# A fused transformer layer with 32 experts on one core: landing places for two down units instead of one gate-up unit, and the expert of fewest tokens processed last

## The reference

```python
logits = (xt @ p['w_router']).astype(F32) + p['b_router'].astype(F32)
topv, topi = lax.top_k(logits, TOP_K)
wts = jax.nn.softmax(topv, axis=-1)
...
gu = xb @ p['w_gu'][e] + p['b_gu'][e]
gate = jnp.minimum(gu[:, :D_FF], SWIGLU_LIMIT)
up = jnp.clip(gu[:, D_FF:], -SWIGLU_LIMIT, SWIGLU_LIMIT)
act = (up + 1.0) * gate * jax.nn.sigmoid(SWIGLU_ALPHA * gate)
return (act @ p['w_down'][e] + p['b_down'][e]).astype(F32) * w[:, None]
```

## Time and profile before

| | us |
|---|---|
| median of 3 runs | 1631.74 (1631.41 to 1634.96) |
| the profiled execution | 1629.55, span 1627.9 |
| PE, DVE, ACT, POOL busy | 1403.2, 624.3, 247.6, 183.9 |
| DMA | 505.66 MB, mean 311 GB/s |

### The profile page before, as it was taken

The page is one execution under the profiler, slowest core; times in us unless marked ns, Lnnn a source line. Parts: engine busy times, 40 slices in busy tenths (PEclk is TensorE's granted clock), DMA queues, the critical chain, the costliest instruction groups (busy, mean ns, idle before and its releaser), DMA issues.

```text
span 1627.9 us, 40564 instructions
## 1 busy us (share of the span) xinstructions
PE 1403.2 (86%) x16361; PEld 758.5 (47%) x16362; DVE 624.3 (38%) x1321; ACT 247.6 (15%) x580; POOL 183.9 (11%) x240
## 2 busy tenths in 40 slices
PE   6998989999999699979999797797779797779794
PEld 3445656367676445535554353343335343334352
DVE  2334646344623534334344242332314332233334
ACT  2124532211110311101111010000001010000011
POOL 2021310000000001000110110110110110001100
PEclk9999989988999699989999898898989898899897
DMA  9734992940191379699999999999999969997940
GB/s 356 247 137 151 356 396 72 369 150 1 46 351 69 155 307 408 266 402 423 406 395 403 428 414 417 417 406 415 414 424 407 413 283 393 423 407 295 384 183 33
DMA packets 71426, 505.66 MB, mean 311 GB/s; under 512 B 6528, under 2 KB 6648, under 8 KB 35316
## 3 DMA queue, kind: packets, MB, share of 16 engines
q1 hardware_dynamic: 63588, 480.98, 73.1%
q0 software_dynamic: 7792, 24.08, 4.5%
HBM read 499.92 MB, written 5.11 MB: 310 GB/s over the span
## 4 chain that ended last, share of the span: by engine, by line
PE 72%; DMA 17%; DVE 6%; issue 1%; ACT 1%; POOL 1%; SPq 1%; DVEq 0%; ACTq 0%; POOLq 0%
PE psum L533 67%; DMA region<-in_w_gu 13%; DMA ring<-in_w_down 2%; PE psum L697 2%; DMA ring<-in_w_ada 2%; PE psum L1018 1%; PE psum L993 1%; DVE region L1315 1%; POOL ring L2208 1%; DMA ring<-in_w_gu 1%; DVE region L1164 1%; PE psum L729 0%; ACT region L1819 0%; DVE region L1282 0%; SPq L2273 0%
## 5 line engine op out<-in xcount | busy, mean ns | idle before, releaser
L533 PE MATMUL psum<-ring,region 128*32 128x256 f32 (+2 forms) x11264 | 744.6, 390 | 138.1 <-POOL ring L2208 134.1
L533 PEld LDWEIGHTS psum<-ring,region 128*32 128x32 f32 (+1 forms) x11264 | 370.5, 112 | 460.2 <-POOL ring L2208 165.6
L1819 ACT ACTIVATE region<-psum 128x256 f32<-128x256 f32 (+5 forms) x330 | 136.7, 417 | 1149.5 <-PE psum L533 503.6
L533 PE MATMUL psum<-region 128*32 128x256 f32 (+11 forms) x2700 | 253.2, 424 | 19.1 <-DVE region L1208 9.0
L2208 POOL COPY ring<-region 128x1024 f32<-128x1024 f32 x124 | 123.8, 1041 | 919.7 <-DMA region<-in_w_gu 744.4
L1729 DVE TENSOR_TENSOR region<-region,psum 128x1280 f32<-128x1280 f32 x110 | 163.2, 1484 | 165.8 <-PE psum L533 165.8
L533 PE MATMUL psum<-region,ring 128*128 128x320 f32 (+1 forms) x640 | 170.3, 421 | 1.4 <-DVE region L1570 1.4
L1699 DVE TENSOR_SCALAR region<-psum,region 128x320 f32<-128x320 f32 x55 | 30.3, 551 | 355.7 <-PE psum L533 355.7
L533 PEld LDWEIGHTS psum<-region 128*32 128x32 f32 (+5 forms) x2700 | 101.5, 138 | 129.3 <-issue 91.8
L533 PEld LDWEIGHTS psum<-region,ring 128*128 128x128 f32 x640 | 117.2, 193 | 48.8 <-issue 5.5
L1685 DVE TENSOR_SCALAR region<-region 128x32 f32<-128x32 f32 x168 | 34.7, 266 | 106.0 <-issue 106.0
(11 more groups left out here) (301 smaller groups left out, 769.5 us busy)
## 6 DMA issues: line engine op xcount, KB each, us to landing
ring<-in_w_gu SPq DMA_DIRECT2D x97, 2048.0 KB, 11.3
ring<-in_w_down SPq DMA_DIRECT2D x64, 2048.0 KB, 11.3
region<-in_w_gu SPq DMA_DIRECT2D x31, 2048.0 KB, 17.3
ring<-in_w_ada SPq DMA_DIRECT2D x12, 2048.0 KB, 13.8
ring<-in_w_in SPq DMA_DIRECT2D x11, 2048.0 KB, 19.3
ring<-in_cache_k SPq DMA_DIRECT2D x64, 256.0 KB, 5.0
ring<-in_cache_v POOLq DMA_DIRECT2D x64, 256.0 KB, 5.2
ring<-in_w_out SPq DMA_DIRECT2D x2, 2048.0 KB, 21.3
```

Of the source, the lines that this page charges most:

```text
L533: return pe.matmul(out, lhsT, rhs, start=start, stop=stop, skip_group_check=True)
L1819: return act.activation(out, src, ACT.Copy)
```

## The change

- `LANDINGS` becomes 2, and the landing places are those of the two down units (4 and 5) instead of quarter 0. The second place lies in space of the router's scratch; the tiles that live on beside it are laid out below it.
- SP's order for an expert becomes: quarters 0, 1, 2 and 3 of this expert into the ring, each behind its wait, then for each down unit a wait until GpSimd has moved all four pieces of *this* expert's unit, and the fill of the *next* expert's. Its first fill of the second place waits for the last readers of the scratch.
- TensorE waits for quarter 0 as for the others (one semaphore, no pieces) and before each down unit for that unit's fourth piece.
- GpSimd copies two units an expert, eight pieces instead of four.
- The expert with fewest tokens among experts 2 to 31 is processed last; those behind it move up by one. For this DVE finds the least count, makes a step number for each expert, TensorE turns it, and the running sums are made in the new order; lists `AT_STEP` (step of a block, for the semaphore counts) and `AT_ORDER` (expert of a step, for SP's loads) are added.
- SP reads three registers an expert instead of one.

```diff
-LANDINGS = 1
+LANDINGS = 2
...
+        landing = [region[:, REGION + KT * NT - UNIT:REGION + KT * NT], Area(E.at).take(UNIT)]
...
-            pe.wait_ge(blocks_ready, 1)
+            pe.wait_ge(steps_ready, 1)
+            out = claim(pe, ALLB, "steps")
+            mm(out[0:NE, 0:NE], ones[0:1, 0:NE], step_row[0:1, 0:NE], True, True)
+            mm(out[0:NE, NE:NE + 1], step_row[0:1, 0:NE], ones[0:1, 0:1], True, True)\
+                .then_inc(full_sem("steps"), 1)
+            pe.wait_ge(reached_ready, 1)
...
             def gate_up_quarter(c, expert):
 
-                if c >= LANDINGS:
-                    pe.wait_ge(unit_landed[moe_slot[c]], 16 * expert + (landed_base[c] + 16))
+                pe.wait_ge(unit_landed[moe_slot[c]], 16 * expert + (landed_base[c] + 16))
...
-                        if c < LANDINGS:
-                            pe.wait_ge(piece_moved[c], PIECES * expert + (2 * j + q + 1))
...
             def down(expert):
                 for half in range(2):
                     i = 4 + half
-                    pe.wait_ge(unit_landed[moe_slot[i]], 16 * expert + (landed_base[i] + 16))
+                    pe.wait_ge(piece_moved[half], PIECES * expert + PIECES)
...
+            step(dve.memset(least_row[0:1, :], -4.0 * NT))
+            dve.tensor_scalar(least_row[0:1, 2:NE], pp[0:1, 162:160 + NE], -1.0, None, ALU.mult)
...
+            step(dve.max(least8[0:1, :], least_row[0:1, :]))
+            step(dve.max_index(least_ix[:], least8[0:1, :], least_row[0:1, :]))
+            step(dve.tensor_copy(step_row[0:1, 2 * NE:2 * NE + 1], least_ix[:, 0:1]))
+            least = step_row[0:1, 2 * NE:2 * NE + 1]
+            step(dve.scalar_tensor_tensor(step_row[0:1, 0:NE], iota[0:1, 0:NE], least, iota[0:1, 0:NE],
+                                          ALU.is_gt, ALU.subtract))
+            step(dve.tensor_scalar(step_row[0:1, NE:2 * NE], iota[0:1, 0:NE], least, -float(NE),
+                                   ALU.is_equal, ALU.mult))
+            step(dve.tensor_tensor(step_row[0:1, 0:NE], step_row[0:1, 0:NE], step_row[0:1, NE:2 * NE], ALU.add))
+            dve.tensor_scalar(step_row[0:1, 0:NE], step_row[0:1, 0:NE], -1.0, float(NE - 1), ALU.mult, ALU.min)\
+                .then_inc(steps_ready, 1)
+            dve.wait_ge(*own(steps_ready))
+            dve.wait_ge(*full("steps"))
+            step(dve.tensor_copy(step_of[0:NE, 0:1], bank("steps")[0:NE, NE:NE + 1]))
+            dve.tensor_scalar(reached[0:NE, 0, :], bank("steps")[0:NE, 0:NE], step_of[0:NE, 0:1], None, ALU.is_ge)
...
                 for i in range(LANDINGS):
-                    pool.wait_ge(unit_landed[moe_slot[i]], landed_base[i] + 16)
-                    pool.wait_ge(unit_read[i], before)
+                    pool.wait_ge(unit_landed[moe_slot[4 + i]], landed_base[4 + i] + 16)
+                    pool.wait_ge(unit_read[4 + i], before)
                     pool.wait_ge(landing_filled[i], filled)
...
-                sp.dma_start(landing[i], gu[expert, i].rearrange("o p f -> p (o f)")).then_inc(landing_filled[i], 16)
+                sp.dma_start(landing[i].rearrange("p (c f) -> p c f", c=2),
+                             dn[expert, i].rearrange("o p c f -> p (o c) f")).then_inc(landing_filled[i], 16)
...
-                    elif i < LANDINGS:
+                    elif i >= RING - LANDINGS:
                         continue
...
+            for m in range(KT):
+                sp.wait_ge(*drained("bd", m))
+            sp.wait_ge(weight_rows_ready, 1)
+            fill_landing(1, slice(1, 2))
             with sp.Fori(1, NE - 1) as e:
                 before = sp.value_load(ints[0:1, bass.ds(e + (AT_BLOCKS - 1), 1)], min_val=1,
                                        max_val=MAX_BLOCKS)
-                expert_weights(bass.ds(e, 1), before)
+                this = sp.value_load(ints[0:1, bass.ds(e + AT_ORDER, 1)], min_val=0, max_val=NE - 1)
+                after = sp.value_load(ints[0:1, bass.ds(e + (AT_ORDER + 1), 1)], min_val=0, max_val=NE - 1)
+                expert_weights(bass.ds(this, 1), before)
                 for i in range(LANDINGS):
                     sp.wait_ge(piece_moved[i], PIECES * e + PIECES)
-                    fill_landing(i, bass.ds(e + 1, 1))
+                    fill_landing(i, bass.ds(after, 1))
```

More of the change, by code:

```diff
@@ L65 @@
 AT_ROUND = AT_LATER + 1
-N_INTS = AT_ROUND + N_LIST
+AT_STEP = AT_ROUND + N_LIST
+AT_ORDER = AT_STEP + N_LIST
+N_INTS = AT_ORDER + NE
 def const_pack():
@@ L265, in build @@
         selwT = E.take(NT)
+        pos = E.take(3, ROUNDS * NE)
         E.at = max(E.at, fin_at + KT * NT + 2 * FF)
         late_const = E.take(n_const - n_late)
+        wts = E.take(3, NE)
+        fin_ss = E.take(6)
+        fin_rstd = E.take(3)
+        plan_row = E.take(N_LIST)
+        fin_gain = E.take(D)
+        landing = [region[:, REGION + KT * NT - UNIT:REGION + KT * NT], Area(E.at).take(UNIT)]
         logits = E.take(3, NE)
         mask = E.take(3, NE)
-        wts = E.take(3, NE)
         eq = E.take(3, NE)
@@ L286, in build @@
         begun = E.take(N_LIST)
[L287 to L290, removed]
+        active = E.take(N_LIST)
+        least_row = E.take(NE)
+        least8 = E.take(8)
+        step_row = E.take(2 * NE + 1)
+        step_of = E.take(3)
+        reached = E.take(3, NE)
         x1_sq = Area(REGION - KT * NT).take(KT, NT)
-        landing = [region[:, REGION + KT * NT - UNIT:REGION + KT * NT]]
         assert E.at <= REGION - KT * NT
-        pos = E.take(3, ROUNDS * NE)
+        assert E.at <= REGION + KT * NT - UNIT
         y_out = h2_tok
         top_ix = sb("top_ix", [P, 3, 8], U32)
+        least_ix = sb("least_ix", [1, 8], U32)
         spare = hmT[:].rearrange("p h t -> p (h t)").bitcast(BF16)
@@ L936, in _ @@
             for i in range(3):
-                last = mm(out[0:NE, 128:129], mask[:, i, :], ones[:, 0:1], i == 0, i == 2)
+                mm(out[0:NE, 128:129], mask[:, i, :], ones[:, 0:1], i == 0, i == 2)
+            for i in range(3):
+                last = mm(out[0:1, 160:160 + NE], ones[:, 0:1], mask[:, i, :], i == 0, i == 2)
             last.then_inc(full_sem("pos"), 1)
@@ L968, in _ @@
             mm(out[0:1, 0:N_LIST], ones[0:NE, 0:1], begun[0:NE, :], True, True)
-            mm(out[0:1, P:P + N_LIST], plan[0:NE, 0:1], begun[0:NE, :], True, True)\
+            mm(out[0:1, P:P + N_LIST], plan[0:NE, 0:1], begun[0:NE, :], True, True)
+            mm(out[0:1, 2 * P:2 * P + N_LIST], const("number", NE), active[0:NE, :], True, True)\
                 .then_inc(full_sem("list"), 1)
@@ L1653, in _ @@
             step(dve.tensor_reduce(plan[0:NE, 1:2], plan[0:NE, 2:1 + ROUNDS], AX, ALU.add))
-            dve.tensor_scalar(plan[0:NE, 0:1], plan[0:NE, 1:2], 1.0, None, ALU.add).then_inc(blocks_ready, 1)
-            dve.wait_ge(*own(blocks_ready))
+            step(dve.tensor_scalar(plan[0:NE, 0:1], plan[0:NE, 1:2], 1.0, None, ALU.add))
+            step(dve.max(least8[0:1, :], least_row[0:1, :]))
[13 more added lines that the diff above has]
+            dve.tensor_scalar(reached[0:NE, 0, :], bank("steps")[0:NE, 0:NE], step_of[0:NE, 0:1], None, ALU.is_ge)
+            dve.tensor_scalar(reached[0:NE, 1, :], iota[0:NE, 0:NE], step_of[0:NE, 0:1], None, ALU.is_ge)\
+                .then_inc(free_sem("steps"), 1)
+            dve.wait_ge(*drained("steps"))
+            dve.tensor_scalar(reached[0:NE, 2, :], iota[0:NE, 0:NE], step_of[0:NE, 0:1], None, ALU.is_equal)\
+                .then_inc(reached_ready, 1)
+            dve.wait_ge(*own(reached_ready))
             dve.tensor_copy(split_f32[:, NT:2 * NT], bank("wT")[0:3 * NE, 0:NT]).then_inc(free_sem("wT"), 1)
@@ L1663, in _ @@
             dve.wait_ge(*drained("cum"))
+            step(dve.tensor_tensor(step_of[0:NE, 2:3], plan[0:NE, 1:2], plan[0:NE, 0:1], ALU.subtract))
+            step(dve.tensor_scalar(active[0:NE, :], iota[0:NE, 0:N_LIST], step_of[0:NE, 2:3], None, ALU.is_ge))
+            step(dve.scalar_tensor_tensor(active[0:NE, :], iota[0:NE, 0:N_LIST], plan[0:NE, 1:2], active[0:NE, :],
+                                          ALU.is_lt, ALU.mult))
             dve.tensor_scalar(begun[0:NE, :], iota[0:NE, 0:N_LIST], plan[0:NE, 1:2], None,
@@ L1675, in _ @@
             dve.scalar_tensor_tensor(ints[0:1, AT_COLUMN:AT_COLUMN + N_LIST], plan_row[0:1, :],
-                                     float(NE), ls[0:1, 0:N_LIST], ALU.mult, ALU.add)\
+                                     float(NE), active[0:1, :], ALU.mult, ALU.add)\
                 .then_inc(free_sem("list"), 1)
@@ L2207, in _ @@
                         part = slice(UNIT // PIECES * piece, UNIT // PIECES * (piece + 1))
-                        pool.tensor_copy(ring[:, moe_slot[i], part], landing[i][:, part])\
+                        pool.tensor_copy(ring[:, moe_slot[4 + i], part], landing[i][:, part])\
                             .then_inc(piece_moved[i], 1)
```

30 lines of the change are left out of this document (20 added, 10 removed).

## The result

The changed kernel takes 1661.54 us (median of 4 runs, 1660.03 to 1665.48), the kernel before 1631.96 in the runs beside it: 1.0184 times as long, 95% interval 1.0168 to 1.0200. The forecast was 1647.8. Its direction and its mechanism hold; in size, +16 was forecast and +30 came. The profiled execution after took 1660.03, span 1658.4, 30.5 more than the span before.

The account below looks back on a forecast made before the run. DMA was taken to bound one-block experts, TensorE those of two and three. Terms of +17.1 (cycle), +2.6 (after three blocks), +6.5 (start) and -10.1 (order) gave +16.1 us on 1631.7: 1647.8 us, range 1621 to 1670.

Parts of the forecast that it names:

- What bounds the kernel: Expert stage: one-block experts bound by DMA (29.5 us against 15.6), two-block (31.1 against 29.5) and three-block (46.7) by TensorE.
- (1) The cycle: Refill loop of each expert: one-block steps go from 29.5 to 31.4 us, two-block from 31.1; +17.1 from expert 5 to 24.
- A: Time mark: start of the second quarter (quarter 1) in an expert's first block, from which the loop's steps are counted.
- (2) After three blocks: One-block expert after a three-block one, queue empty: next second quarter 32.9 us after its start, before 30.3; +2.6 for expert 4.
- (3) The start: Start of the kernel: new table work delays the block list by 3.6 us; with expert 1's loads the start costs +6.5.
- (4) The order: Expert 24 to the last block's end, expert 25 moved behind 31: 276.5 us instead of 286.6, -10.1; order alone -13.9.
- S: Time mark: start of the one-block expert that follows a three-block expert.
- The registers: SP's loop: three register loads instead of one take at most some 2.5 us more an expert, hidden.
- The doubled GpSimd work: GpSimd in the expert stage: 124 more copies of 1.04 us cost nothing of themselves beyond the refill loop.
- A, the bubble doesn't appear: Rival: fills land in under 6.9 us, steps stay 29.5 and 31.12; -3 to -9 or -24 us, middle 1624; chance 0.25.
- B, slower copies: Rival: GpSimd copies beside DVE work take 5 us for four instead of 4, each step 1 us longer: 1672; chance 0.08.
- C: Rival: the least expert has two blocks or none is moved, so the order loses 13.9 us: 1662; chance 0.03.

Follow-up runs that it names:

- e9_more_registers: The changed kernel with two more register loads in each turn of SP's loop (five an expert): 1662.97 us against 1661.5 for the change.
- e8_half_fills: The changed kernel with each down fill split into two of 1 MB, the first issued when two of four pieces are moved, all copies whole: 1637.95 us.
- e1_order_only: The kernel before with only the new expert order and its tables, one landing place for quarter 0 kept: 1624.68 us, 0.9944 of the kernel before.
- e3_short_copy: The changed kernel with GpSimd's copies cut from 1024 to 64 columns a piece, all waits, fills and loads kept: 1629.79 us.

## Why the forecast was right in kind and short in size

**What bounds the kernel: held.** TensorE's work is the same, the stream's share fell, and the experts go by whichever of the two is longer.

**(1) The cycle.** The reading was right link by link: copies from A + 3.8, 7.92 us for eight, fill at A + 8.0 (forecast 7.9), landing after 8.3 us in the median (taken 8.6), median step 31.4 (forecast 31.4), with 15 of the 19 steps between 31.1 and 32.1. That an ordinary step came out at 31.4 is in part luck: the latency was 0.3 us shorter than taken, and the sum had no hole ahead of the second fill, where there are 0.5 us. Four steps, those from experts 5, 11, 18 and 20, took 33.4 to 33.6, and these are what the term lacked: together 8.3 us over 31.4, of the 9.4 that were missed. One of them is 738.02 to 771.59 above. The run of 96 products in it and in the step after, from TensorE's timeline, with the windows of the same two runs (and of the wait ahead of the first), GpSimd's copies and SP's fills behind them:

```profile
738.02 7.60 PE L546 MATMUL psum<-ring,region 128*32 128x256 f32 x96 [0.63 <-DMA ring<-in_w_gu]
...
771.59 5.39 PE L546 MATMUL psum<-ring,region 128*32 128x256 f32 x96
```

```profile
724.00:738.00 14.00, 4.27 (x34) 1.67 (x34) 0.46 (x4) 0.38 (x1) 0.00 (x0) 0.50 1.01 431
738.00:743.50 5.50, 5.48 (x60) 2.61 (x64) 0.00 (x0) 0.00 (x0) 0.00 (x0) 0.59 1.01 429
...
771.60:777.00 5.40, 5.40 (x97) 3.10 (x98) 0.66 (x4) 0.29 (x1) 1.60 (x2) 1.00 1.02 434
```

```profile
744.06 7.92 POOL L2259 COPY ring<-region 128x1024 f32<-128x1024 f32 x8 [25.54 <-PE psum L546]
...
775.40 7.92 POOL L2259 COPY ring<-region 128x1024 f32<-128x1024 f32 x8 [23.43 <-PE psum L546]
```

```profile
748.21 4.32 SPq L2306 DMA_DIRECT2D region<-in_w_down  x2
...
779.56 4.31 SPq L2306 DMA_DIRECT2D region<-in_w_down  x2
```

In the 14 us ahead of expert 5's A TensorE worked for 4.27 and was granted 0.50 of its clock, the lower of its two levels (1.2 and 2.4 GHz). In the 5.5 us behind A it was granted 0.59, so mostly still the lower level, and the 96 products took 7.60 us instead of 5.39. So the down unit was read late, the copy began at A + 6.0 instead of A + 3.8, and the fill went out at A + 10.2 instead of A + 8.0, 2.2 us late at both links. The first fill then landed faster (7.5 us after its issue instead of 8.1) and the second that much later behind it, so the next A is late by 2.2 us all the same. Before, such a start cost nothing, because the first down load was issued with 9.8 us still queued: there too the clock fell, to 0.81 to 0.87 in the 5.5 us behind the landing of quarter 1 of experts 14, 16 and 18, and the next quarter 1 landed 29.5 to 29.8 us later.

The forecast took "3.57 us to the read" for every expert; the step that failed is that one number, which the change had turned from a covered time into a link of the loop. No run takes the clock's part away, but two traces show it apart from the rest. After, the clock in the 5.5 us behind A is 0.59 to 0.66 in the four long steps and 1.00 in the fifteen others. `e9_more_registers`, the same kernel but for hidden register loads, has five low starts there (0.59 to 0.68), with steps of 33.1 to 33.6 us, and expert 5, granted 1.00 this time, has a step of 31.3 instead of 33.6. From that trace, the chain of waits and the window behind this A:

```profile
738.71 11.81 PE psum L546 x194
...
770.02 11.81 PE psum L546 x194
```

```profile
738.70:744.20 5.50, 5.50 (x98) 3.13 (x98) 0.00 (x0) 0.00 (x0) 1.68 (x2) 1.00 1.00 429
```

What decides that a start is slow isn't shown: ahead of expert 14's A in the trace after the clock was 0.50 just so (1012.5 to 1026), and behind it 1.00.

**(2) After three blocks: +3.4, forecast +2.6.** Mechanism right: the first fill, issued at A + 7.9 into an idle queue, landed 7.6 us later as priced. The second landed 5.8 us after it instead of 4.9, and that is the 0.8.

**(3) The start: +8.7, forecast +6.5.** The tables came as counted, 3.1 against 3.6. 0.9 us lay ahead of them (the first routed product starts at 558.56 instead of 557.64); that says little, since in the traces of kernels with the same tables this start lies anywhere from 556.4 (`e8_half_fills`) to 561.2 (`e1_order_only`). The rest is one thing left out: the first fill of the second landing place, new in SP's queue and waiting for the readers of the scratch, is issued at 578.3, ahead of expert 1's quarter 0 at 581.5, and that quarter lands 10.3 us after its issue. The forecast took 9.0 us and didn't count this transfer of 4.9 us in front of the quarter.

**(4) The order: -7.8, forecast -10.1.** Two restarts from an empty queue lie in this stretch, priced at S + 32.9. In the chain of waits they take 34.0 us (1388.31 to 1422.30) and 33.7 (1529.28 to 1563.00), which is 1.9 of the 2.3 missed; as in (2), the second fill landed late, here 6.3 and 5.9 us after the first. By the runs the order is a gain of 11 to 16 us, on both sides of the 13.9 forecast.

**Hidden edits.** The registers: held (`e9_more_registers`). The doubled GpSimd work: it is no part of the 23.6 us that came back with it in place (`e8_half_fills`); that it costs nothing at all isn't shown, for up to 8 us.

**The rivals.** A, the bubble doesn't appear: fell; no fill landed in under 6.9 us. By the figures that the Trainium skill states (DMA: Bandwidth & Descriptors, "Anatomy of one DMA — SWDGE (gpsimd) path") the estimate was 6.8 us and the stream would have held; the measured 7.4 at the least decides against it here. The section gives these figures for DMAs that GpSimd issues, and SP issues these, which the prediction left out when it used them. B, slower copies: fell, 1041 ns over 248 copies. The contention that the Trainium skill states (GPSIMD Engine Reference, "Specifications") is with VectorE instructions that have two inputs in SBUF or are in a 2-port mode. The prediction held against it, but the addition there (`region,psum`) has one of its inputs in PSUM, and so has every VectorE instruction that ran beside a copy in the trace after (L1748, L1751 and L1779). So the 1041 ns decide against B, and that contention wasn't put to the test here. C fell: expert 25 stands behind 31 in one block.

**What it was for.** Even with the copy nearly free (`e3_short_copy`, 1629.8) two places for down units are no faster than one for quarter 0 with the same order (1624.7). An expert of one block needs 29.5 us for its bytes and one of three is bound by TensorE; an extra unit of lead changes neither. That explanation of the 5 us rests on the argument and was not taken further apart; the start alone is part of it, since both landing-place kernels have the extra fill there.

## What to carry to other kernels

When a staging place takes the place of a direct load, write out the whole loop of one refill (read, copy, issue, issue to landing) and hold it against the bytes that are queued at that moment; a link of 4 us in an in-order queue is worth its full length less that cover, and once the cover is gone every jitter of an earlier link counts too. Issuing a part of the refill as soon as a part of the place is empty won back 23.6 of the 36.9 us with one edit. Where loads bind some jobs and compute others, put a load-bound job behind the longest compute-bound one (11 to 16 us for one expert here); and before one unit is read earlier, look which unit is then read later, since its refill may be the next to be late.

## What the runs showed of the hardware that was not expected

The time from issue to landing of one 2 MB load rose from 7.4 to 7.6 us on an idle queue to 8.4 when the load ahead of it had 1.8 us left to run, and to 10.3 when it had 4.9. By the idle figure 7.6 us would have been enough in the second case. One load of the kernel before took 10.0 with 2.5 left, so what is left isn't all that sets it. A load issued before the queue ran dry still left a hole. A low granted clock (0.59 over 5.5 us) made 96 products 2.2 us longer, and through the loop that clock cost DMA time. A fill issued by GpSimd took 0.71 us of its time and 0.67 us of waiting ahead of it, where SP's fills cost GpSimd nothing.
